# Gate and up of the second feed-forward with high and low inputs side by side in one product of 512 columns

## What is computed

```python
def swiglu(h, w_gate, w_up, w_down):
    return (jax.nn.silu(h @ w_gate) * (h @ w_up)) @ w_down

x = post(x, swiglu(pre(x, mod_l, 2, g_pre[l, 2]), w2_gate[l], w2_up[l], w2_down[l]), mod_l, 2, g_post[l, 2], 0.5)
```

## Time and profile before

| | |
|---|---|
| median of 3 runs | 3304.87 us |
| the profiled execution | 3300.94 us, span 3299.1 us |
| TensorE matmul busy | 3104.7 us (94%), 21174 matmuls |
| VectorE busy | 1810.7 us (55%) |
| ScalarE busy | 1030.7 us (31%) |
| mean granted TensorE clock | 0.976 of full speed |
| HBM read | 497.55 MB |

### The profile page before, as it was taken

The page is one execution under the profiler, slowest core; times in us unless marked ns, Lnnn a source line. Parts: engine busy times, 40 slices in busy tenths (PEclk is TensorE's granted clock), DMA queues, the critical chain, the costliest instruction groups (busy, mean ns, idle before and its releaser), DMA issues. The chain is left out here.

```text
span 3299.1 us, 50736 instructions
## 1 busy us (share of the span) xinstructions
PE 3104.7 (94%) x21174; PEld 2665.1 (81%) x21174; DVE 1810.7 (55%) x2184; ACT 1030.7 (31%) x1298; POOL 11.9 (0%) x18
## 2 busy tenths in 40 slices
PE   6899999999999999999599998999888999999997
PEld 3588878878887787887378897777768999999996
DVE  3346556555565565655644645665346555555554
ACT  3222122122222212212532452222355444444433
POOL 0000000000000000000000000000000000000000
PEclk9999999999999999999899999999898999999998
DMA  9735445444464665755123440000434555555551
GB/s 322 270 108 184 153 141 185 141 159 140 153 204 164 219 229 184 274 203 192 67 78 101 134 150 12 2 2 2 155 112 141 178 179 181 182 174 180 184 179 64
DMA packets 323470, 501.73 MB, mean 152 GB/s; under 512 B 7964, under 2 KB 244004, under 8 KB 307716
## 3 DMA queue, kind: packets, MB, share of 16 engines
q1 hardware_dynamic: 321792, 494.73, 44.5%
q0 software_dynamic: 704, 4.62, 0.4%
q10 hardware_dynamic: 836, 0.33, 0.0%
HBM read 497.55 MB, written 2.10 MB: 151 GB/s over the span
## 5 line engine op out<-in xcount | busy, mean ns | idle before, releaser
L1800 PE MATMUL ps<-xn,parts 128*128 128x256 f32 (+1 forms) x11184 | 1900.9, 332 | 59.3 <-DVE xn L1413 50.3
L1800 PEld LDWEIGHTS ps<-xn,parts 128*128 128x128 f32 x11184 | 1693.2, 191 | 268.3 <-DVE xn L1413 32.3
L1199 DVE TENSOR_TENSOR parts<-raw,parts 128x1024 fp32r<-128x1024 f32 x642 | 768.9, 1221 | 571.0 <-ACT parts L650 570.5
L650 ACT ACTIVATE parts<-raw 128x1024 fp32r<-128x1024 f32 x640 | 664.9, 1055 | 1189.4 <-PE ps L1800 967.7
L1800 PE MATMUL ps<-h_parts,parts 128*128 128x512 f32 (+1 forms) x4224 | 742.2, 337 | 26.7 <-DVE h_f L1255 25.2
L1800 PEld LDWEIGHTS ps<-h_parts,parts 128*128 128x128 f32 x4224 | 648.5, 190 | 120.5 <-issue 35.9
L1276 DVE TENSOR_TENSOR acc<-acc,ps 128x256 f32<-128x256 f32 (+1 forms) x336 | 184.2, 548 | 308.7 <-PE ps L1800 308.5
L1219 DVE SCALAR_TENSOR_TENSOR macc<-raw,cs,macc 128x2048 f32<-128x2048 f32 x150 | 348.1, 2345 | 0.0
L1255 DVE TENSOR_TENSOR h_f<-silu_g,ps 128x512 f32<-128x512 f32 (+1 forms) x42 | 39.5, 942 | 223.9 <-PE ps L1800 223.9
L660 ACT ACTIVATE h_parts<-h_f 128x512 fp32r<-128x512 f32 (+1 forms) x42 | 35.1, 836 | 333.2 <-DVE h_f L1255 333.2
L1800 PE MATMUL ps<-sq_buf,c 128*128 128x256 f32 (+1 forms) x160 | 64.1, 518 | 17.2 <-ACT sq_buf L773 12.5
(11 more groups left out here) (199 smaller groups left out, 1252.3 us busy)
## 6 DMA issues: line engine op xcount, KB each, us to landing
raw<-in_w_mod SPq DMA_DIRECT2D x144, 1024.0 KB, 6.3
raw<-in_w_gate SPq DMA_DIRECT2D x88, 1024.0 KB, 5.1
raw<-in_w_up SPq DMA_DIRECT2D x88, 1024.0 KB, 5.1
raw<-in_w_down SPq DMA_DIRECT2D x88, 1024.0 KB, 5.1
raw<-in_w_in SPq DMA_DIRECT2D x41, 1024.0 KB, 5.3
raw<-in_w_out SPq DMA_DIRECT2D x16, 1024.0 KB, 5.5
x_in<-in_ctx SPq DMA_DIRECT2D x2, 1024.0 KB, 6.7
x_in<-in_x SPq DMA_DIRECT2D x2, 1024.0 KB, 12.0
```

Source lines behind the costliest of these rows:

```text
L650: nc.scalar.activation(parts[:, unit % PART_SLOTS, 0, :], raw[:, slot, b * UNIT:(b + 1) * UNIT], ACT.Copy).then_inc(hi_ready, 1)
L1199: nc.vector.tensor_tensor(parts[:, pslot, 1, :], raw[:, slot, b * UNIT:(b + 1) * UNIT], parts[:, pslot, 0, :].bitcast(F32), ALU.subtract)\
L1800: return nc.tensor.matmul(o, lhsT, rhs, start=start, stop=stop)
```

## The change

In the gate and up products of the second feed-forward (N = SEQ), two of the three products of a K tile share the high weight: with the high and with the low input. They become one matmul whose moving operand is both inputs, 2 x 256 = 512 columns, and which fills a whole PSUM bank: columns 0 to 255 hold the sums with the high input, 256 to 511 those with the low input. The third product (low weight, high input) is added into columns 0 to 255. So each bank then holds two halves that have to be added. VectorE does this by a tensor_reduce over pairs that lie 256 columns apart (`halves`), 1024 elements in and 512 out: for a gate half into `silu_g` at u = 4 and 12, for an up half into `h_f32` at u = 8 and 16. Silu and the multiplication then read SBUF, Silu in place. Two semaphores are new: `g_sum`, for which ScalarE waits ahead of the Silu, and `u_sum`, for which VectorE waits itself ahead of the multiplication. The first feed-forward, the projections and the down products stay as they are.

```diff
+        def halves(bank):
+            return ps[:, bank:bank + 2, :].rearrange("p b (e n) -> p b n e", e=2)
...
@@ ScalarE, ffn_round
                     if u in (4, 12):
                         s = u // 12
-                        act.wait_ge(units_done, ubase + u)
                         act.wait_ge(h_ok, 2 * G + s + 1)
-                        nc.scalar.activation(silu_g[:, :, 0:N], ps[:, 4 * s:4 * s + 2, 0:N],
-                                             ACT.Silu).then_inc(silu_ok, 1)
+                        if N == SEQ:
+                            act.wait_ge(g_sum, 2 * (G - ROUNDS) + s + 1)
+                            gate_in = silu_g[:, :, 0:N]
+                        else:
+                            act.wait_ge(units_done, ubase + u)
+                            gate_in = ps[:, 4 * s:4 * s + 2, 0:N]
+                        nc.scalar.activation(silu_g[:, :, 0:N], gate_in, ACT.Silu).then_inc(silu_ok, 1)
...
@@ VectorE, ffn_round
                 for u in range(24):
+                    if u in (4, 12) and N == SEQ:
+                        s = u // 12
+                        dve.wait_ge(units_done, ubase + u)
+                        dve.wait_ge(h_ok, 2 * G + s + 1)
+                        nc.vector.tensor_reduce(silu_g[:, :, 0:N], halves(4 * s), axis=mybir.AxisListType.X, op=ALU.add).then_inc(g_sum, 1)
                     if u in (8, 16):
                         s = u // 8 - 1
                         dve.wait_ge(units_done, ubase + u)
+                        up = 2 if s == 0 else 0
+                        if N == SEQ:
+                            nc.vector.tensor_reduce(h_f32[:, :, 0:N], halves(up), axis=mybir.AxisListType.X, op=ALU.add).then_inc(u_sum, 1)
+                            dve.wait_ge(u_sum, 2 * (G - ROUNDS) + s + 1)
+                            up_in = h_f32[:, :, 0:N]
+                        else:
+                            up_in = ps[:, up:up + 2, 0:N]
                         dve.wait_ge(silu_ok, 2 * G + s + 1)
-                        up = 2 if s == 0 else 0
-                        nc.vector.tensor_tensor(h_f32[:, :, 0:N], silu_g[:, :, 0:N], ps[:, up:up + 2, 0:N],
-                                                ALU.mult).then_inc(h_ok, 1)
+                        nc.vector.tensor_tensor(h_f32[:, :, 0:N], silu_g[:, :, 0:N], up_in, ALU.mult).then_inc(h_ok, 1)
...
@@ TensorE
+            def side_by_side(bank, slot, c0, act, k, start, stop):
+                w_hi, w_lo = parts[:, slot, 0, c0:c0 + P], parts[:, slot, 1, c0:c0 + P]
+                mm(ps[:, bank, :].rearrange("p (e n) -> p e n", e=2), w_hi, act[:, :, k, :], start, False)
+                return mm(ps[:, bank, 0:SEQ], w_lo, act[:, 0, k, :], False, stop)
...
+                        if twin:
+                            last = side_by_side(banks[nt], slot, 256 * kk + P * nt, a, k, k == 0, k == KT - 1)
+                            continue
```

More of the change, by code:

```diff
@@ L335, in build_layer @@
         in_copied = sem("in_copied")
+        g_sum, u_sum = sem("g_sum"), sem("u_sum")
         def chunk_src(w, rows, r0, n_rows, col, n_cols):
@@ L1817, in three, with wide_unit @@
                 return mm(o, w_lo, act_hi, False, stop)
-            def wide_unit(seg, i, j, b, banks, N, a):
+            def side_by_side(bank, slot, c0, act, k, start, stop):
+                w_hi, w_lo = parts[:, slot, 0, c0:c0 + P], parts[:, slot, 1, c0:c0 + P]
+                mm(ps[:, bank, :].rearrange("p (e n) -> p e n", e=2), w_hi, act[:, :, k, :], start, False)
+                return mm(ps[:, bank, 0:SEQ], w_lo, act[:, 0, k, :], False, stop)
+            def wide_unit(seg, i, j, b, banks, N, a, twin=False):
                 slot = unit_ready(seg, i, j, b)
@@ L1921, in ffn_round @@
                     for b in range(2):
-                        wide_unit(seg, i, j0 + j, b, banks, N, a)
+                        wide_unit(seg, i, j0 + j, b, banks, N, a, N == SEQ)
                 for j in range(4):
```

## The result

The changed kernel takes 3316.57 us, the median of 7 runs (3315.49 to 3318.88), against 3303.13 us for the kernel before in the same series (7 runs, the three of the start among them): 13.4 us more, ratio 1.0040 with an interval of 1.0028 to 1.0052. The forecast was 7.0 us more than the 3304.87 us of the start, 3311.9 us.

A forecast was written before the change was run, and what follows sets the result against it. TensorE was taken to bound the second feed-forward's 11 rounds, each its products plus one pause. Products -18.8, pause +13.8 and clock falls +12.0 gave +7.0 us on the median 3304.87: 3311.9 us, range 3298 to 3325.

The forecast's parts named there:

- The reduction: VectorE's new PSUM reduction before the last multiplication of a round: 1.22 us for 1024 inputs, bounds 1.07 and 1.88.
- The rival of the slow read: Jumping PSUM read makes the reduction 1.88 us and the pause 2.85 us: +17.5 us, 3322.4 us; chance 0.26.
- The pause: TensorE's wait before each round's down projection grows from 0.94 to 2.19 us: 13.8 us more over 11 rounds.
- The clock: After the longer pauses the granted clock falls to half level in 8 of 11 rounds, 1.5 us each: 12.0 us more.
- The mixer's four in five: In the mixer, four of five TensorE pauses of 1.75 to 2.08 us preceded a clock of 0.83; basis for 8 falls.
- The first rival (the clock holds): No clock falls follow the longer pauses in the second feed-forward: sum -5.0 us, 3299.9 us; chance 0.17.
- The products: Gate and up triples become 512 + 256 columns, 360.0 to 346.7 ns each: 18.8 us less over 1408 triples.
- the bound named for the unknown (two pieces): Wide product's operand as two distant pieces in xn2: taken at no cost, bounds 0 and 13.3 ns a triple.
- The third rival (no gain): Two pieces cost the fixed 13.3 ns again, so the wide product's 18.8 us are gone: 3330.7 us; chance 0.04.
- The sum: Whole change: -18.8 + 13.8 + 12.0 = +7.0 us, giving 3311.9 us.
- The covers named for the gate reductions: Three more reductions a round, 3.7 us on VectorE, stay hidden from TensorE; tightest slack 0.6 us at unit 10; cost nothing.

The follow-up runs named there:

- e2: Changed kernel, but the second feed-forward's down projection starts before the second half is multiplied, waiting for it in its second unit: 3290.14 us, ratio 0.9962.
- e4: Kernel before plus a reduction of 1024 PSUM elements ahead of the second half's multiplication, products still three of 256 columns: 3320.36 us, ratio 1.0054.
- e7: As e4, plus 8 unused products of 256 columns in the middle of each round's gate and up products: 3336.38 us, ratio 1.0099.
- e11: Changed kernel with the down projection started early and the low weight also multiplied by both inputs, all gate and up products 512 columns: 3434.37 us, single run.
- e1: Changed kernel with high and low parts of a K tile side by side in SBUF, so wide products read 512 straight columns: 3317.73 us, ratio 1.0048.
- e10: Changed kernel with early down projection, each unit's products grouped by width, and high and low parts side by side in SBUF: 3287.72 us, ratio 0.9958.

## Why the prediction was right, and where not

**The reduction.** 1.22 us forecast, 1.224 measured: the read out of PSUM that jumps at every element goes at the rate of a straight one (1221 ns). The rival of the slow read falls. Of the two figures of the Trainium skill (Vector Engine (DVE) Microarchitecture Reference, 5.2 Measured stream behaviour) the one for a source that alternates between two regions holds here too, for PSUM.

**The pause.** 2.19 us forecast, 2.13 measured; 13.0 us for 13.8.

**The clock.** The step held: eight falls of 1.5 us were forecast, seven came, 1.5 us each. e2 shows that they go with the pause. The number itself was luck in part. The mixer's four in five gave the right number for this kernel; with a pause as long, e4 had one in 11 and e7 six. With one fall, as in e4, the change would have cost some 4 us instead of 13. The first rival (the clock holds) fell with this. So did the rule of the Trainium skill (TensorE: Matmul & The Clock Gate, Why this matters for your kernels), which warns only of longer gaps: here the granted clock fell after 2.13 us.

**The products.** This is the mis-sized term. 13.3 ns a triple and 18.8 us were forecast; 360.0 - 353.1 = 6.9 ns came in ten rounds, 0.84 us a round, and the forecast 1.7 us in the first round alone: 10.1 us in all. The two paces, 226.7 and 120.0 ns, were each read from stretches in which all products have one width, and adding them assumed that a product takes the same beside one of another width. e11 shows that 226.7 holds in this place too, as long as no other width stands between; e1 and e10 show that the bound named for the unknown (two pieces) was the wrong one. The third rival (no gain) was half true, by another mechanism.

**The sum.** -10.1 + 13.0 + 10.5 - 0.9 (low clock at the entry) = +12.5 us against +7.0. The missing 8.7 us of the products are larger than the whole difference; the other terms came out 3.2 us lower than forecast. The covers named for the gate reductions held: TensorE waits for no split and for no Silu.

## What to carry to other kernels

A product that is saved on the busiest engine can be worth less than nothing if the work that replaces it falls into the pause that ends a stage; look first whether the wait behind that pause is needed at that place. Here moving that one wait was worth 11.6 us by itself, and with the rest of the longer chain hidden too the change became worth doing. A pace read from uniform stretches holds for uniform stretches: before two widths are mixed, the mixture has to be timed.

## What the runs showed of the hardware

- Matmuls of 512 and of 256 columns in turn: 353.1 ns a pair, where 226.7 + 120.0 = 346.7 would be the sum of their paces among their own kind. In groups of four, 2.5 ns of the difference come back. In one round of 11 the pair took 346.6 ns; why is open.
- A moving operand of two pieces costs nothing measurable (pieces of 68.53 us a round with and without).
- Pauses of TensorE of 1.67 us brought no fall of the granted clock from 2.4 to 1.2 GHz in 11 rounds; pauses of 2.1 to 2.2 us brought 7, 7, 1 and 6 in 11 in four kernels (changed kernel, e1, e4, e7). Each fall lasted 3.4 us and cost 1.4 to 1.5 us.
- Ten pauses of 1.48 us, once gone, gave back 1.8 us each, and eleven of 0.94 us 1.2 us each.
- A tensor_reduce over pairs 256 columns apart in PSUM, 1024 elements to 512, takes 1.224 us.
